# Hybrid encoder block: value columns of the recurrence taken 512 at a time, in half pieces, with the first two in a later slot

## The reference

```
u = _rmsnorm(h, attn_norm_w[layer])
proj = jnp.einsum('bsd,de->bse', u, w_in[layer])
qa, ka, va, hq, hff, hfb, hi, hg = jnp.split(proj, split_idx, axis=-1)
y_na = _neighbourhood_attention(qa, ka, va, q_norm_w[layer], k_norm_w[layer], rpb[layer], rows)
y_hg = _hgrn2_bidirectional(hq, hff, hfb, hi, hg, lbf_all[layer], lbb_all[layer], hg_norm_w[layer])
mix = jnp.concatenate([y_na, y_hg], axis=-1).astype(h.dtype)
h = h + jnp.einsum('bse,ed->bsd', mix, w_out[layer])
u = _rmsnorm(h, mlp_norm_w[layer])
a = jnp.square(jax.nn.relu(jnp.einsum('bsd,df->bsf', u, w_up[layer])))
h = h + jnp.einsum('bsf,fd->bsd', a, w_down[layer])
```

## Time and profile before

| what | us |
|---|---|
| median of 3 runs | 1290.2 |
| lowest, highest | 1288.53, 1290.71 |
| profiled execution, its time | 1288.35 |
| profiled execution, its span | 1286.5 |

### The profile page before, as it was taken

The page is one execution under the profiler, slowest core; times in us unless marked ns, Lnnn a source line. Parts: engine busy times, 40 slices in busy tenths (PEclk is TensorE's granted clock), DMA queues, the critical chain, the costliest instruction groups (busy, mean ns, idle before and its releaser), DMA issues.

```text
span 1286.5 us, 17686 instructions
## 1 busy us (share of the span) xinstructions
PE 1272.7 (99%) x6432; PEld 1072.3 (83%) x6432; DVE 841.7 (65%) x1268; ACT 587.5 (46%) x1058; POOL 475.1 (37%) x259
## 2 busy tenths in 40 slices
PE   7999999999999999999999999999999999999998
PEld 6878888998888889888887888888888888888887
DVE  4637666631859686976486654554545888888885
ACT  6346766445536354350355554354363433433341
POOL 3341212105040503045135555455452544544452
PEclk9999999999999999999999999999999999999999
DMA  8341333222010202152311744444569463533533
GB/s 262 125 120 50 97 93 84 78 66 83 1 50 1 66 1 65 51 196 85 113 49 58 243 152 146 155 146 145 160 219 375 135 229 98 199 128 98 163 88 143
DMA packets 134469, 154.92 MB, mean 120 GB/s; under 512 B 11376, under 2 KB 89584, under 8 KB 134384
## 3 DMA queue, kind: packets, MB, share of 16 engines
q1 hardware_dynamic: 131216, 147.04, 35.6%
q10 hardware_dynamic: 3168, 6.75, 1.4%
HBM read 109.72 MB, written 44.04 MB: 120 GB/s over the span
## 4 chain that ended last, share of the span: by engine, by line
PE 96%; DVE 2%; ACT 1%; issue 1%; DMA 0%; POOL 0%; DVEq 0%; ACTq 0%
PE bank L2332 8%; PE bank L2335 8%; PE bank L2336 8%; PE bank L2363 8%; PE bank L2367 8%; PE bank L2366 8%; PE bank L2073 6%; PE bank L2069 6%; PE bank L2072 6%; PE bank L2156 4%; PE bank L2293 2%; PE bank L2289 2%; PE bank L2292 2%; PE bank L1967 1%; PE bank L1969 1%; PE bank L1968 1%
## 5 line engine op out<-in xcount | busy, mean ns | idle before, releaser
L883 POOL TENSOR_TENSOR w_hi<-stage,one_col 128x1024 fp32r<-128x1024 f32 x32 | 61.3, 1917 | 409.6 <-DVE scores L1615 175.3
L943 POOL TENSOR_TENSOR a_split<-a_raw,a_split 128x1024 fp32r<-128x1024 f32 x56 | 148.0, 2660 | 166.1 <-ACT a_split L1223 166.1
L2332 PE MATMUL bank<-set,w_hi 128*128 128x512 f32 x448 | 177.7, 397 | 0.1
L2335 PE MATMUL bank<-set,w_hi 128*128 128x512 f32 x448 | 176.1, 393 | 0.0
L2336 PE MATMUL bank<-set,w_lo 128*128 128x512 f32 x448 | 176.0, 393 | 0.0
L2363 PE MATMUL bank<-w_hi,a_split 128*128 128x512 f32 x448 | 174.6, 390 | 0.2
L2367 PE MATMUL bank<-w_hi,a_split 128*128 128x512 f32 x448 | 174.3, 389 | 0.0
L2366 PE MATMUL bank<-w_lo,a_split 128*128 128x512 f32 x448 | 174.3, 389 | 0.0
L2069 PE MATMUL bank<-uT_hi,w_hi 128*128 128x512 f32 x384 | 158.8, 413 | 0.0
L2073 PE MATMUL bank<-uT_hi,w_lo 128*128 128x512 f32 x384 | 150.5, 392 | 0.0
L2072 PE MATMUL bank<-uT_lo,w_hi 128*128 128x512 f32 x384 | 149.7, 390 | 0.0
(11 more groups left out here) (227 smaller groups left out, 2743.7 us busy)
## 6 DMA issues: line engine op xcount, KB each, us to landing
a_raw<-a_dram SPq DMA_DIRECT2D x56, 512.0 KB, 3.8
a_dram<-abuf SPq DMA_DIRECT2D x111, 256.0 KB, 2.1
stage<-in_w_in SPq DMA_DIRECT2D x29, 512.0 KB, 4.1
raw<-in_w_down SPq DMA_DIRECT2D x10, 1024.0 KB, 8.2
stage<-in_w_up SPq DMA_DIRECT2D x16, 512.0 KB, 5.6
raw_b<-in_w_up SPq DMA_DIRECT2D x16, 512.0 KB, 5.5
x_tok<-in_x SPq DMA_DIRECT2D x8, 512.0 KB, 8.8
v_dram<-vs ACTq DMA_DIRECT2D x16, 256.0 KB, 2.3
```

The lines of the kernel that those rows point to most:

```text
L943: pool.tensor_tensor(split_of(m, 1), a_raw[:, m % 4, :, :], split_of(m, 0).bitcast(F32), ALU.subtract).then_inc(b_lo, 1)
L2332: first = pe.matmul(dst, w[0], u[0], start=k == 0 and p in (1, 5, 6, 7), stop=False, skip_group_check=True)
L2335: pe.matmul(dst, w[0], u[1], start=False, stop=False, skip_group_check=True)
```

## The change

The unit of `h_v` has a third form, `("hv", 2, t)`, with all 512 columns of a token tile. Token tiles 0 and 1 (`HALF_TOKENS`) keep two units of 256 columns, tiles 2 to 7 have one unit of 512 columns each, and these are cut into two pieces of four slices. There are still 16 pieces in 16 slots: two narrow units, twelve wide half units (12 matmuls of 512 columns each), two narrow units. A wide unit waits for four weight tiles (12 to 15) in place of two, and is evicted once, after its second piece. In step 10 the two pieces stand in slots 1 and 2 in place of 0 and 1, and ACT's evictions move with them. The release of weight tiles 12 and 13 moves from the first unit of the second column half (before in step 12, slot 1) to the same unit's new place, step 15, slot 0. SP's list has the band of step 15 ahead of the load of tile 18, not behind it.

```diff
+HALF_TOKENS, FULL_TOKENS = (0, 1), tuple(range(2, TT))
@@ proj_units
-    u += [("hv", c, t) for c in range(2) for t in range(TT)]
+    u += [("hv", 0, t) for t in HALF_TOKENS] + [("hv", 2, t) for t in FULL_TOKENS] + [("hv", 1, t) for t in HALF_TOKENS]
...
-VALUE_AT = {(s, 2 * i if s == 9 else i): j for s, js in VALUE_UNITS.items() for i, j in enumerate(js)}
-BANDS_BEFORE = {13: (2,), 14: (3, 4), 15: (5, 6), 16: (7, 8), 17: (9, 10), 18: (12, 13, 14), 19: (15,)}
+VALUE_PIECES = [(("hv", 0, t), range(KT)) for t in HALF_TOKENS]
+VALUE_PIECES += [(("hv", 2, t), ks) for t in FULL_TOKENS for ks in (range(4), range(4, KT))]
+VALUE_PIECES += [(("hv", 1, t), range(KT)) for t in HALF_TOKENS]
+VALUE_AT = {(s, 2 * i if s == 9 else i + (s == 10)): j for s, js in VALUE_STEPS.items() for i, j in enumerate(js)}
+BANDS_BEFORE = {13: (2,), 14: (3, 4), 15: (5, 6), 16: (7, 8), 17: (9, 10), 18: (12, 13, 14, 15)}
@@ ACT, unit
-                    if what == 0 and part < NG:
+                    if what != 1 and part < NG:
-                    act.activation(h_v[:, part, 256 * what:256 * what + 256], b[:, 0:256], ACT.Copy).then_inc(act_freed, 1)
+                    c0, w = (0, 512) if what == 2 else (256 * what, 256)
+                    act.activation(h_v[:, part, c0:c0 + w], b[:, 0:w], ACT.Copy).then_inc(act_freed, 1)
@@ ACT, the attention steps
-                values = [UNIT[("hv", 0, 0)] + i for i in VALUE_UNITS.get(s, ())]
-                for n in values[:1] if s > 9 else ():
+                values = [VALUE_PIECES[j] for j in VALUE_STEPS.get(s, ())]
+                values = (s == 10) * [[]] + [[UNIT[u]] if ks[-1] == KT - 1 else [] for u, ks in values] + 4 * [[]]
+                for n in values[0] if s > 9 else ():
                     unit(n)
...
@@ PE, projection
-                    done = 2 * (p1 == TT - 1)
+                    done = 2 * ((UNITS[n - 1][1], p1) in ((2, TT - 1), (1, HALF_TOKENS[-1])))
-                    tile = TILE_OF[("in", C_HV + 256 * what)]
-                    pe.wait_ge(w_split, 2 * (tile + 2))
+                    c0, tiles = (0, 4) if what == 2 else (256 * what, 2)
+                    tile = TILE_OF[("in", C_HV + c0)]
+                    pe.wait_ge(w_split, 2 * (tile + tiles))
-                        w = [t[:, r:r + 2, P * k:P * k + P] for t in ring]
-                        dst = b[:, 0:256]
+                        w = [t[:, r:r + tiles, P * k:P * k + P] for t in ring]
+                        dst = b[:, 0:P * tiles]
@@ PE, share
-                        projection(UNIT[("hv", 0, 0)] + VALUE_AT[(s, i)])
+                        u, ks = VALUE_PIECES[VALUE_AT[(s, i)]]
+                        projection(UNIT[u], ks)
```

More of the change, by code:

```diff
@@ L152 @@
 STEP_UNIT = {s: BEFORE + 1 + s for s in range(-2, 9)}
-VALUE_UNITS = {9: (0, 1), 10: (2, 3), 11: (4, 5, 6), 12: (7, 8, 9), 13: (10, 11), 14: (12, 13), 15: (14, 15)}
-VALUE_AT = {(s, 2 * i if s == 9 else i): j for s, js in VALUE_UNITS.items() for i, j in enumerate(js)}
-BANDS_BEFORE = {13: (2,), 14: (3, 4), 15: (5, 6), 16: (7, 8), 17: (9, 10), 18: (12, 13, 14), 19: (15,)}
+VALUE_PIECES = [(("hv", 0, t), range(KT)) for t in HALF_TOKENS]
+VALUE_PIECES += [(("hv", 2, t), ks) for t in FULL_TOKENS for ks in (range(4), range(4, KT))]
+VALUE_PIECES += [(("hv", 1, t), range(KT)) for t in HALF_TOKENS]
+VALUE_STEPS = {9: (0, 1), 10: (2, 3), 11: (4, 5, 6), 12: (7, 8, 9), 13: (10, 11), 14: (12, 13), 15: (14, 15)}
+VALUE_AT = {(s, 2 * i if s == 9 else i + (s == 10)): j for s, js in VALUE_STEPS.items() for i, j in enumerate(js)}
+BANDS_BEFORE = {13: (2,), 14: (3, 4), 15: (5, 6), 16: (7, 8), 17: (9, 10), 18: (12, 13, 14, 15)}
 WINDOW_BEFORE = {13: 1, 15: 2, 17: 3}
@@ L1278, in _ @@
                     take_pT(s, 2)
-                for n in values[1:2] if s > 9 else ():
+                for n in values[1] if s > 9 else ():
                     unit(n)
@@ L1282, in _ @@
                     take_pT(s, 3)
-                for n in values[2:]:
+                for n in values[2]:
                     unit(n)
@@ L1295, in _ @@
                     if s == 9 and g == 1:
-                        unit(values[0])
+                        unit(values[0][0])
                 if s == 9:
-                    unit(values[1])
+                    unit(values[1][0])
                 if s >= 0:
```

## The result

| | before | after |
|---|---|---|
| median of 17 runs each, us | 1289.9 | 1291.6 |
| lowest, highest | 1288.53, 1290.71 | 1290.65, 1295.47 |
| span of the profiled execution | 1286.5 | 1289.5 |

The ratio of after to before is 1.0019, with a 95% interval of 1.0013 to 1.0026: slower by 1.7 to 3.4 us, inside what the prediction called no change (0.2%), and near its edge. The predicted time was 1291.5 us. The profile says more than the median, and it says that the time was right partly by chance: two mechanisms are at work where the forecast had one.

A forecast was written before the change was run, and what follows sets the result against it. PE's own work bounds the kernel (busy 99%); +2.9 (emptied slot) - 1.4 (wide pieces) - 0.2 (end of step 10) = +1.3 us, giving 1291.5 us against the median of the runs; range 1289.2 to 1294.0 us.

The forecast's parts named there:

- no change: Whole kernel: differences up to about 0.2%, 2.6 us, count as same; chance of same 0.78, slower 0.18, faster 0.04.
- The emptied slot: Step 10, slot 0: PE stands 3.11 us for ACT's mixing, the piece's work is done later in slot 2; +2.9 us.
- the end of the step: Step 10, slots 1 and 2: pieces lie over PE waits of 0.1 us each; about -0.2 us.
- The wide pieces: Twelve narrow units become twelve pieces of 12 wide matmuls, gaining 0.12 us each; -1.4 us, from -1.1 to -1.8.
- the four boundaries: Step boundaries where the shorter slot 0 piece uses up ACT's room of 0.1 us; put at nothing, +0.1 us for the range.
- a sign of being wrong: The forecast counts as wrong if a new wait stands at slot 0 of steps 11 to 14; one of three such signs.
- The clock: TensorE's clock behind the gap in step 10: the forecast's sum has no term for a fall, left to a rival.
- Rival 1: Step 10: TensorE's clock falls in the gap, costing up to 2.4 us more; +3.7 us, 1293.9 us; chance 0.14.
- Rivals 2 and 3: Product waits only for low probabilities: -0.7 us, chance 0.07; wide matmuls bring nothing: +2.7 us, chance 0.07.
- The steps called free: Waiting for tile 15, later release of tiles 12 and 13, last band ahead of tile 18: no cost each.

The follow-up runs named there:

- e2: Kernel before, all 16 units narrow, only the two units of step 10 moved to slots 1 and 2: median 1293.37 us, ratio to before 1.0036.
- f1: Changed kernel with twelve 512-column matmuls, results never read, in empty slot 0 of step 10: median 1291.25 us, ratio to before 1.0012.
- e4: Changed kernel with ACT's mixing of step 9 one exponential and one eviction earlier: median 1288.23 us, ratio to before 0.9988.
- f4: Changed kernel with ACT's mixing of step 9 ahead of the second narrow unit's eviction: median 1290.97 us, ratio to before 1.0020.
- f2: Changed kernel with two more 512-column activations on ACT ahead of the mixing of step 9: median 1293.66 us, ratio to before 1.0036.
- e3: Changed kernel with three narrow token tiles, not two, and slots 0 and 1 of step 10 filled as before: median 1289.7 us, ratio to before 0.9997.
- f3: Three narrow token tiles, step 10's slot 0 filled, ACT's mixing one exponential earlier from step 9 on: median 1289.25 us, ratio to before 0.9994.
- g1: The changed kernel run again unchanged: 1292.0 us in one run, section 73.33 us.
- g2: The changed kernel run again unchanged, a second further execution: 1291.75 us in one run, section 73.33 us.

## Why the prediction was right, and where it was not

**The emptied slot: right.** The forecast let PE stand for the 3.11 us that the slot had taken, and the product came at 226.05, 0.04 us from where it was, with ACT's mixing named. The price of +2.9 us, less 0.2 at the end of the step, was measured alone by e2 as 2.68 us. That no work is saved by an empty slot while a wait behind it doesn't move was the step on which the sign rested.

**The wide pieces: mechanism right, size off.** The term was -1.4 us with 0.12 us a piece. The pieces did take some 0.10 to 0.12 us less (2.83 to 2.85 for 2.94 to 2.97 behind transposes, 2.75 and 2.77 for 2.87 in slot 2). What failed is the step on the four boundaries: "some 0.1 us of room, which the shorter piece in slot 0 uses up and doesn't overrun by more than 0.05". In steps 11 to 14 the product behind slot 0 gave 0.08 us back each time, 0.3 us in all. The term is about -1.1 us, and the sum without the clock +1.6 by f1 and +1.55 by the first profile, against +1.3 forecast. The room itself, 0.26 us from ACT's end to PE's start less the 0.14 us that step 10 showed between the two, was read well: the product starts 0.15 us behind the mixing and the piece ahead of it loses 0.01 us or less. What the sum left out is that a product which starts right behind its release takes 0.43 us in place of 0.35. The kernel before has both: 226.09 to 226.52 in step 10, 236.76 to 237.11 in step 11. That is the new wait at slot 0 of steps 11 to 14 that the prediction had named as a sign of being wrong, though a small one. The pieces' 0.11 to 0.12 us, twelve times, are 1.3 to 1.4 us, 9 to 10 ns for each of the 144 matmuls fewer. By the fixed cost of some 2.5 ns for each matmul that the Trainium skill gives ("TensorE: Matmul & The Clock Gate", section "Wait — 56ns, not 53.3ns?") they would have brought 0.4 us (and the sum +2.3, where the prediction wrote near +2.4), so the rows of the trace were the better guide.

**The clock: this step failed.** The forecast put the clock's term at nothing, and it cost 1.4 to 1.7 us, more than the forecast's whole +1.3. Rival 1 had a chance of 0.14, and its mechanism happened in four profiles out of four with such a stand. Its argument against was that the gap is less than half of the one at the start, which has no bearing: the start shows only that 7 us are enough. Nor was the 1.00 of the earlier trace rows a reading: the kept record of the granted clock in that profile begins at 11.90 us, just where the pace becomes full, and the view prints 1.00 where it has none. No row of before had a stand between 1 and 7 us, so the trace could not say where the fall begins, and the chance should have been near even. Its price, up to 2.4 us, was taken from the start's whole slow stretch, and was too high. The section moved by +3.03 to +3.24 us, nearer to the rival's +3.7 than to the forecast's +1.3.

**Why the time was still right.** The medians lie 1.7 us apart and the ratio says 1.7 to 3.4 us, while the section says 3.0 to 3.2. The median of the kernel before fell by 0.3 us from 3 to 17 runs, and the arrival at the changed place varies by up to 3 us from one execution to the next, which a median of 17 doesn't take out to a few tenths. 1291.5 was near 1291.6 with a part of the cost missing: the sign and the emptied slot were foreseen, the closeness of the number is luck.

**Rivals 2 and 3: out, as weighed.** The mixing sets the wait (e4, f4, f2), and wide matmuls with an operand from four ring slots run at the pace of the others.

**The steps called free were free.** The wide piece in slot 1 didn't wait for tile 15. POOL split tile 16 from 283.52, released by the first narrow unit of step 15, and PE didn't wait for it at the first gate unit (291.82): 

```profile
283.52 1.89 POOL L891 TENSOR_TENSOR w_hi<-stage,one_col 128x1024 fp32r<-128x1024 f32 x1 [59.78 <-PE bank L2067]
285.50 2.40 POOL L894 TENSOR_TENSOR w_lo<-stage,w_hi 128x1024 fp32r<-128x1024 f32 x1
```

## What to carry to other kernels

A piece of filler work between two waits is worth what it covers, not what it costs: before moving it, look which chain ends just as it ends, even where the profile labels no wait, by comparing the slot's length (3.11 us) with its usual one (2.96 us). If an empty stand of TensorE can't be avoided, keep it short, or put work of any kind into it; here one narrow unit left in the slot (e3) took the section from 3.0 us over the kernel before to 0.8 us under it, and the earlier mixing beside it (f3) to 1.4 us under. Where executions differ by more than the effect, compare a section of the trace between two instructions that both kernels have.

## What the hardware showed unexpectedly

In the profiles TensorE's granted clock fell to 1.2 GHz behind stands of 2.86, 2.87 and 4.19 us and held at 2.4 GHz behind 2.60 and 1.16 us. By the mean clocks of other runs it is not the length alone that decides: behind 2.60 us it seems to have fallen in two of eight runs (f4), and behind 2.86 us it seems to have held in some (e2). In the first profile and in f2 it was low already when work began again; in e2, g1 and g2 it was full for the product and fell within the next piece, in g1 1.1 us after the product's start. The Trainium skill ("TensorE: Matmul & The Clock Gate", section "Why this matters for your kernels") warns against idle gaps between bursts; the trace agrees.

A wide matmul with its moving operand in four pieces of 128 columns, 4096 bytes apart, runs at the 0.227 to 0.232 us of the earlier trace rows. Two narrow ones take 0.239 us, so that twelve wide ones in place of twelve pairs bring 0.11 us.
